# Both RMS norms of the second block: half squares, an earlier first tile, transposes inside products, and 512 wide features made by token tile

## The reference, cut to what matters

```python
def rmsnorm(x, g):
    y = x * lax.rsqrt(jnp.mean(x * x, axis=-1, keepdims=True) + 1e-6)
    return y * g

xn = rmsnorm(x, norm_mix)                 # first norm, tag (2, 1)
q, k_..., v_..., u_rnn, gates = jnp.split(xn @ w_in, cuts, axis=-1)
merged = ...                              # recurrent branch and attention branch
h = x + merged @ w_out                    # 1024 x 1024, "out"
z = rmsnorm(h, norm_mlp) @ w_mlp_in       # second norm, tag (2, 2); 1024 x 4096
return h + jnp.square(jax.nn.relu(z)) @ w_mlp_out
```

## Time and profile before

| | us |
|---|---|
| median of three runs | 1648.37 |
| the profiled execution | 1646.42 |
| its span on the core | 1644.6 |
| TensorE busy | 1554.4 (95%) |
| VectorE busy | 1031.8 (63%) |
| ScalarE busy | 796.1 (48%) |
| GpSimd busy | 230.0 (14%) |

### The profile page before, as it was taken

The page is one execution under the profiler, slowest core; times in us unless marked ns, Lnnn a source line. Parts: engine busy times, 40 slices in busy tenths (PEclk is TensorE's granted clock), DMA queues, the critical chain, the costliest instruction groups (busy, mean ns, idle before and its releaser), DMA issues.

```text
span 1644.6 us, 25103 instructions
## 1 busy us (share of the span) xinstructions
PE 1554.4 (95%) x10311; PEld 1395.9 (85%) x10311; DVE 1031.8 (63%) x1704; ACT 796.1 (48%) x1427; POOL 230.0 (14%) x189
## 2 busy tenths in 40 slices
PE   9999999898998999989899998899988799989999
PEld 6899889698986889989789986788876699979987
DVE  5765595685855675477578765455754486646643
ACT  4545445364642455444456652453446564435531
POOL 2300121211202120032021100012010040100000
PEclk9999999999999989999999999999999799989999
DMA  8633355359564533255355564455211144535553
GB/s 315 225 103 116 93 213 194 141 178 209 185 227 156 192 114 129 78 180 205 104 179 181 184 208 158 158 187 190 82 45 62 64 156 151 200 123 185 180 181 126
DMA packets 41026, 261.32 MB, mean 159 GB/s; under 512 B 4512, under 2 KB 5152, under 8 KB 14672
## 3 DMA queue, kind: packets, MB, share of 16 engines
q1 hardware_dynamic: 35600, 238.44, 42.0%
q0 software_dynamic: 2944, 15.69, 3.7%
q10 hardware_dynamic: 2368, 5.58, 0.9%
HBM read 254.98 MB, written 4.19 MB: 158 GB/s over the span
## 4 chain that ended last, share of the span: by engine, by line
PE 76%; DVE 11%; ACT 5%; issue 3%; DMA 3%; POOL 1%; ACTq 0%; DVEq 0%; POOLq 0%; SPq 0%
PE ps L482 68%; PE ps L588 3%; DVE lows L1522 3%; DMA raw<-d_wst 2%; PE ps L669 1%; ACT wh L1014 1%; ACT S L1434 1%; DVE ar L2038 1%; PE ps L690 1%; POOL sm L2220 1%; DVE S L2100 1%; PE ps L584 0%; PE ps L708 0%; DVE xTr L1541 0%; ACT xTr L1035 0%
## 5 line engine op out<-in xcount | busy, mean ns | idle before, releaser
L1522 DVE TENSOR_TENSOR lows<-raw,wh 128x1024 fp32r<-128x1024 f32 (+3 forms) x473 | 545.4, 1172 | 263.4 <-ACT wh L1014 260.8
L482 PE MATMUL ps<-xTr,wh 128*128 128x256 f32 (+1 forms) x3536 | 649.2, 286 | 11.4 <-DVE lows L1522 7.8
L482 PEld LDWEIGHTS ps<-xTr,wh 128*128 128x128 f32 (+1 forms) x3536 | 552.6, 192 | 16.5 <-issue 9.3
L1014 ACT CAST wh<-raw 128x1024 fp32r<-128x1024 f32 (+3 forms) x473 | 455.3, 990 | 191.7 <-DMA raw<-d_wst 162.4
L482 PE MATMUL ps<-xTr,lows 128*128 128x256 f32 (+1 forms) x1768 | 502.8, 284 | 0.0
L482 PEld LDWEIGHTS ps<-xTr,lows 128*128 128x128 f32 (+1 forms) x1768 | 338.7, 192 | 0.0
L482 PE MATMUL ps<-wh,arR 128*128 128x512 f32 x928 | 298.6, 401 | 4.0 <-DVE ar L1695 4.0
L482 PEld LDWEIGHTS ps<-wh,arR 128*128 128x128 f32 x928 | 176.7, 190 | 49.3 <-DVE ar L1695 5.7
L482 PE MATMUL ps<-lows,arR 128*128 128x512 f32 x464 | 185.3, 399 | 0.0
L482 PE MATMUL ps<-wh,xTr 128*128 128x512 f32 x448 | 146.0, 403 | 16.2 <-DVE xTr L1541 9.3
L482 PE MATMUL ps<-arR,wh 128*128 128x256 f32 (+1 forms) x832 | 148.4, 281 | 0.0
(11 more groups left out here) (261 smaller groups left out, 1553.7 us busy)
## 6 DMA issues: line engine op xcount, KB each, us to landing
raw<-d_wst SPq DMA_DIRECT2D x196, 1024.0 KB, 4.9
raw<-d_wst SPq DMA_DIRECT2D x24, 512.0 KB, 3.5
raw<-d_wst SPq DMA_DIRECT2D x12, 896.0 KB, 4.5
raw<-d_wst SPq DMA_DIRECT2D x8, 672.0 KB, 4.7
ar<-d_lnp POOLq DMA_DIRECT2D x5, 1024.0 KB, 5.1
raw<-d_wst SPq DMA_DIRECT2D x8, 441.0 KB, 3.5
d_scr<-PT POOLq DMA_DIRECT2D x1, 3072.0 KB, 36.0
ar<-d_par POOLq DMA_DIRECT2D x2, 1192.0 KB, 9.5
```

What stands on the lines that cost most here:

```text
L482: op = e.matmul(out, s, m, start=start and i == 0, stop=stop and i == len(pairs) - 1)
L1014: e.copy(high_of(m), raw_of(m)).then_inc(*high.done(m))
L1522: e.tensor_tensor(low_of(m), raw_of(m), high_of(m).bitcast(F32), ALU.subtract).then_inc(*low.done(m))
```

## The change

First norm: the squares are taken by halves, into two sums (scaled by 1/32 before squaring) that the variance adds. DVE interleaves tile 0's RMS norm with tile 1's layer norm; the low parts leave `rms_scaled` and are made by `stream_split` after both halves are scaled. `warm(1)` goes. ACT casts the q2 pieces before tile 0's high parts. POOL's roots follow the new order.

Second norm: tile 0's transposes stand inside the last part of `out`, before its last two row groups; `warm(2)` and `warm(5)` go. The first 512 of the 4096 wide features are made by `tokens_by_tile` ("mlp4"), tile 1's transposes inside its `tile(0)`, before the last piece. ACT copies the two results to SBUF (`mb`), and each of features 0 to 3 is then two transposes, taken alternately with the products of features 4 to 7.

TensorE and the shared definitions:

```diff
+        mb = ar[:, 0:1024].rearrange("p (i c) -> p i c", i=2)
+        mlp_order = [4, 0, 5, 1, 6, 2, 7, 3, *range(8, 32)]
...
-                def tile(i):
+                def tile(i, turn=None):
...
+                        if turn and a == 6:
+                            turn()
...
-            def down(name, key, rw, Y, ready, tail=4):
+            def down(name, key, rw, Y, ready, tail=4, turn=None):
...
                         for p in kept:
+                            if turn and i and h and p[0] == kt - 2:
+                                turn()
                             part(*p, i, h)
...
             tile(0)
-            warm(1)
             stream_turned(tag, 1, xn[1], scaled)
...
-            down(("out", 2), ("w_out_2", 0), RW, merged2, lambda k, i: (vec, "m2l", k))
             tag = (2, 2)
-            warm(2)
-            stream_turned(tag, 0, xn[0], scaled)
-            warm(5)
-            stream_turned(tag, 1, xn[1], scaled)
-            for n in range(32):
+            down(("out", 2), ("w_out_2", 0), RW, merged2, lambda k, i: (vec, "m2l", k),
+                 turn=lambda: stream_turned(tag, 0, xn[0], scaled))
+            tile = tokens_by_tile(("mlp4",), ("w_mlp_in_2", 0), span(0, 512), lambda i: x_ready(tag)[2 * i:2 * i + 2], (act, "mlp4"))
+            tile(0, turn=lambda: stream_turned(tag, 1, xn[1], scaled))
+            product.also("stock", 2, 2)
+            tile(1)
+            for n in mlp_order:
+                if n < 4:
+                    b = M.take(w, ("mlp", n), act, "relu", n)
+                    for i in range(2):
+                        w.wait_ge(act, "mlp4", i)
+                    turned(("mlp", n), [b[:, i * 128:(i + 1) * 128] for i in range(2)],
+                           [mb[:, i, n * 128:(n + 1) * 128] for i in range(2)])
+                    continue
                 features(("mlp", n), ("w_mlp_in_2", 0), 8, 128, RW, span(n * 128), X, x_ready(tag), act, "relu", n)
```

ScalarE, first norm (`squares` takes a half h of a tile now, in both norms):

```diff
             tag = (2, 1)
-            squares(tag, 0, (vec, "ln", 1, 3, 0, 1))
+            for h in range(2):
+                squares(tag, 0, h, vec, "ln", 1, 3, 0, h)
+            highs_of("q2", 0, far=0)
             stream_split(tag, 0, (product, "up", 1, 2 * NZ - 1))
-            squares(tag, 1, (vec, "ln", 1, 3, 1, 1))
-            highs_of("q2", 0, far=0)
+            for h in range(2):
+                squares(tag, 1, h, vec, "ln", 1, 3, 1, h)
```

ScalarE, second norm:

```diff
-            squares2(0)
+            first, *others = pieces.of["mlp4",]
+            highs(first, far=0)
+            for h in range(2):
+                squares(tag, 0, h, vec, "res", "out", 2, 0, h)
+            squares(tag, 1, 0, vec, "res", "out", 2, 1, 0)
             stream_split(tag, 0, (product, "g2", 1, 7))
-            squares2(1)
+            squares(tag, 1, 1, vec, "res", "out", 2, 1, 1)
+            for n in others:
+                highs(n, far=0)
             stream_split(tag, 1, (product, "g2", 1, 7))
+            n = others[-1] + 1
+            highs(n, far=pieces.splits[cast[0]] + 1 - n, count=product.at["stock", 2, 2])
+            for i in range(2):
+                w.wait_ge(product, "mlp4", i)
+                e.copy(mb[:, i, :], M["mlp4", i][:, :]).then_inc(*act.done("mlp4", i))
```

VectorE, first norm (`averaged`, `centred` and `rooted` are the layer norm's `gained` in three parts; the low halves are gone from `rms_scaled`):

```diff
+            normed(last, name, 1.0, 0)
+            for h in range(2):
+                residual(last, name, 1.0, 1, h)
             rms_var(tag, 0)
+            for h in range(2):
+                moments(last, name, 1, h)
+            averaged(last, 1)
             rms_scaled(tag, 0)
+            centred(last, 1)
+            stream_split(tag, 0)
+            rooted(last, 1)
+            lows_for("q2", 0, far=0)
             rms_var(tag, 1)
-            lows_for("q2", 0, far=0)
             rms_scaled(tag, 1)
+            stream_split(tag, 1)
```

VectorE, second norm:

```diff
+            for h in range(2):
+                residual2(0, h)
+            lows_due(others[0], far=0)
+            rms_var(tag, 0)
+            rms_scaled(tag, 0)
+            residual2(1, 0)
+            stream_split(tag, 0)
+            residual2(1, 1)
+            lows_due(others[1], far=0)
+            rms_var(tag, 1)
+            rms_scaled(tag, 1)
+            lows_due(others[2], far=0)
+            stream_split(tag, 1)
```

More of the change, by code:

```diff
@@ L1480, in scalar @@
             tag = (2, 2)
[L1482 to L1486, removed]
-            squares2(0)
+            first, *others = pieces.of["mlp4",]
[3 more added lines that the diff above has]
+            squares(tag, 1, 0, vec, "res", "out", 2, 1, 0)
             stream_split(tag, 0, (product, "g2", 1, 7))
-            squares2(1)
+            squares(tag, 1, 1, vec, "res", "out", 2, 1, 1)
+            for n in others:
+                highs(n, far=0)
             stream_split(tag, 1, (product, "g2", 1, 7))
[L1492 to L1497, removed]
+            n = others[-1] + 1
[3 more added lines that the diff above has]
+                e.copy(mb[:, i, :], M["mlp4", i][:, :]).then_inc(*act.done("mlp4", i))
+            for p, n in enumerate(mlp_order):
+                s = p % 8
+                if n < 4:
+                    w.wait_ge(cross, "mlp", n)
+                else:
+                    highs_of("mlp", n)
+                    w.wait_ge(product, "mlp", n)
+                if p >= 8:
+                    w.wait_ge(vec, "z2l", mlp_order[p - 8])
                 else:
@@ L1563, in gained, with centred @@
                 e.tensor_scalar(ve_, mv[:, 1:2], 1e-5, None, ALU.add).then_inc(*vec.done("var", *tag, i))
+            def centred(tag, i):
+                x = xt(i)
+                mv = list(norm_smalls(i))[1]
                 w.wait_ge(ln_in[tag])
@@ L1566, in gained, with rooted @@
                                        ALU.mult).then_inc(*vec.done("gain", *tag, i))
+            def rooted(tag, i):
+                x = xt(i)
+                rs = list(norm_smalls(i))[4]
                 w.wait_ge(vec, "gain", *tag, i)
@@ L1572, in gained @@
                                            ALU.add).then_inc(*vec.done("ln", *tag, i, h))
+            def gained(tag, i):
+                averaged(tag, i)
+                centred(tag, i)
+                rooted(tag, i)
             def normed(tag, name, scale, i):
@@ L1882, in vector @@
                 tag = (l, 3)
[L1883 to L1886, removed]
+                if l + 1 < DEPTH:
                     normed_by_tile(tag, ("dn", l), 1.0, ("kv", l + 1), ("stock", l, 3))
             def rms_var(tag, i):
-                ss, ve_, rs = rms_smalls(i)
+                ss, ve_, rs, s1 = rms_smalls(i)
                 w.wait_ge(act, "ss", *tag, i)
-                e.tensor_scalar(ve_, ss, 1.0 / 1024, 1e-6, ALU.mult, ALU.add).then_inc(*vec.done("rvar", *tag, i))
+                e.tensor_scalar(ve_, ss, s1, 1e-6, ALU.add, ALU.add).then_inc(*vec.done("rvar", *tag, i))
             def rms_scaled(tag, i):
@@ L2189, in vector, with residual2 @@
             tag = (2, 2)
[L2190 to L2198, removed]
-                lows_for("mlp", n)
-                for m in ([n - 1] if n else []) + ([31] if n == 31 else []):
-                    r = r_[:, m % 8, :]
+            first, *others = pieces.of["mlp4",]
+            lows_due(first, far=0)
+            def residual2(i, h):
+                xh = xt(i)[:, h * 512:(h + 1) * 512]
+                w.wait_ge(product, "out", 2, i, h)
+                e.scalar_tensor_tensor(xh, M["out", 2, i, h][:, :], 0.5, xh, ALU.mult, ALU.add).then_inc(*vec.done("res", "out", 2, i, h))
+            for h in range(2):
[11 more added lines that the diff above has]
+            stream_split(tag, 1)
+            n = others[-1] + 1
+            lows_due(n, far=pieces.splits[left[0]] + 1 - n, count=product.at["stock", 2, 2])
+            for p, n in enumerate(mlp_order):
+                if n >= 4:
+                    lows_for("mlp", n)
+                for m in ([mlp_order[p - 1]] if p else []) + ([31] if n == 31 else []):
+                    r = r_[:, mlp_order.index(m) % 8, :]
                     w.wait_ge(act, "relu", m)
@@ L2307, in gpsimd, with root, rms_root @@
                     e.dma_start(grow, lnp_d[6][:, 0:1024]).then_inc(*gain_in[2, 1].done())
-                roots((l, 3))
                 if l == 0:
+                    roots((l, 3))
                     next_gains((0, 3), 3, (1, 1))
-            def rms(tag):
-                for i in range(2):
-                    ss, ve_, rs = rms_smalls(i)
-                    w.wait_ge(vec, "rvar", *tag, i)
-                    inverse_root(rs, ve_).then_inc(*pool.done("rrs", *tag, i))
+            def root(tag, i):
+                st, mv, nm, ve_, rs, nr = norm_smalls(i)
+                w.wait_ge(vec, "var", *tag, i)
+                inverse_root(rs, ve_).then_inc(*pool.done("rs", *tag, i))
+            def rms_root(tag, i):
+                ss, ve_, rs, s1 = rms_smalls(i)
+                w.wait_ge(vec, "rvar", *tag, i)
+                inverse_root(rs, ve_).then_inc(*pool.done("rrs", *tag, i))
             def first_block_done():
```

(4 more changed lines are left out.)

31 lines of the change are left out of this document (14 added, 17 removed).

## The result

The changed kernel takes 1628.71 us (median of four, 1628.21 to 1631.80) against 1647.34 for the kernel before on the same chip (four, 1643.23 to 1649.96): a ratio of 0.989, 95% interval 0.9865 to 0.9915. That is 18.1 us less by the ratio (14 to 22). The forecast was 1625.7 us, in a range of 1621 to 1632, and 22.7 us less.

The account below looks back on a forecast made before the run. TensorE, busy 95% of the span, was taken as the bound, so only its idle, useless or slow-clock time counts. First norm -10.65 and second norm -12.05 gave -22.7 on 1646.42, 1623.7; the median's 1.95 made 1625.7 us, range 1621 to 1632.

Parts of the forecast that it names:

- First norm, -10.65: First norm, down product to the end of q2's tile 1: ends at 1038.3 against 1048.95, 10.65 us less.
- the warming as the cover: First norm: `warm(6)` holds TensorE to 1021.74 and hides tile 0's norm, with 0.9 us to spare.
- Second norm up to tile 1: Second norm, through mlp4's tile 1: ends at 1457.05, where the kernel before stood at 1470.95 after four features.
- The waits stood at the places named: mlp4's tile 0: TensorE idles 1.0 us before it, 0.95 before piece 2, 0.65 before the last piece.
- Four pairs, 0.85: Features: the 512 token-major features need four pairs of transposes, 0.21 us of TensorE each, 0.85 us added.
- The alternation's second price, 1.0: Feature loop: ACT and DVE turn in 2.98 us against TensorE's 2.88; stock used up near feature 21, 1.0 us of waits.
- the clock falls once: At one of the two norms: 6.4 us at half rate cost 3.2 us, total 1628.9; chance 0.17.
- A fall of the clock was also named as a sign of being wrong: The prediction expected granted clock 1.00 in both q2 tiles and called itself wrong if the clock falls.
- The rule weighed there: Stretches before the tiles: transposes don't count as clock activity; 2.65 and 2.8 us in the first norm, 2.0 at most in the second.
- Each pair costing a whole turn of the loop (6.9 us): Features: each transposed feature costs ACT and DVE a whole 2.98 turn, 6.9 us more, total 1632.6; chance 0.10.
- The inserted transposes had their operand: Rival, both norms: inserted transposes lack their operand and the second tile is late, 1 to 1.5 us each, 1628.4; chance 0.12.
- The weight ring: Features and final product: mlp4 holds half the four weight groups, loads land late, 24 us in all, 1650; chance 0.02.

Follow-up runs that it names:

- Experiment 1: Only the first norm's part of the change, second norm and features as in the kernel before but for squares by halves: 1633.67 us, 0.9923.
- experiment 6: The changed kernel without the six warm products after the first norm's down product: 1631.41 us, 0.9909.
- experiment 9: The changed kernel with squares by whole rows again in both norms: 1627.38 us, 0.9866.
- Experiment 7: The changed kernel with ScalarE casting the third mlp4 piece before the second half of tile 1's squares in the second norm: 1624.13 us, 0.9869.
- experiment 10: The changed kernel with VectorE squaring before low parts, third mlp4 piece cast early, four warm products, tile 0's high parts before tile 1's first squares: 1620.14 us, 0.9830.
- experiment 3: The changed kernel with VectorE squaring the previous feature before making the next low part in the feature loop: 1622.26 us, 0.9852.
- experiment 5: The changed kernel without token-major features: tile 1's transposes follow the out product, then 32 plain features: 1628.77 us, 0.9886.
- experiment 2: Only the second norm's part of the change, first norm's order as in the kernel before, squares by halves: 1637.80 us, 0.9949.

## Why the prediction was right, and where a term was not

The time fell into the range and the direction was right. But it fell there 4.6 us short of the gain that was forecast: two terms came out 0.9 better, and one 5.4 worse. The terms, in the order of the forecast (from the profiled executions):

- **First norm, -10.65: measured -10.96** (21.57 us from the down product to the end of tile 1, against 32.53). Tile 0 at 7.80 (forecast 8.0), tile 1 at 16.03 (16.3), clock 1.00, the warming as the cover: each as forecast. Experiment 1 puts 10 to 15 us on this part, experiment 6 shows what the cover is for. Half squares took 0.63 + 0.19 where 0.59 + 0.19 was taken, and experiment 9 that it didn't matter.
- **Second norm up to tile 1: 0.6 better than forecast.** From the inserted transposes to tile 1's end 16.91 us (1431.94 to 1448.85), forecast 17.55. The waits stood at the places named, but were 0.63, 0.53 and 0.48 and not 1.0, 0.95 and 0.65. Experiment 7 shows the cause of the last two and experiment 10 that of the first: ScalarE's order.
- **Four pairs, 0.85: as forecast**, 3.09 from pair to pair.
- **The alternation's second price, 1.0: this is the term that was mis-sized; it measured 6.4.** The forecast read the loop of 2.98 us against TensorE's 2.88 rightly, and said that the rest would wait "for 1.0 in all" from about feature 21 on. TensorE's ten last features do run 2.98 apart (1501.54 to 1531.33), 1.0 us. But it followed only one product of the loop, the low parts that the features need. The same loop also empties PSUM. When the features end, ScalarE is behind with two relus, TensorE turns to the final product, which wants their banks, and nothing spreads that lag any more: 2.35 us. Behind it the clock fell: 3.1 us.
- **The clock.** The rival "the clock falls once" had the right size (3.2 us against 3.1) for the wrong place, so that its 1628.9 is so near 1628.7 is luck. It was meant for the stretches ahead of the tiles, and all four of those kept full clock. A fall of the clock was also named as a sign of being wrong, and it came, at the start of the final product, where no term and no rival looked for it. The rule weighed there (the Trainium skill, "TensorE: Matmul & The Clock Gate", Part 4: PE-mode transpose: a transpose doesn't count as busy in the same way) isn't decided by these stretches, since none of them lost the clock.
- **The rivals that did not come.** Each pair costing a whole turn of the loop (6.9 us): the pairs took 4.2 us of the loop for two features, as the forecast's 1.25 has it, though the stall it feared came by the banks. The inserted transposes had their operand. The weight ring never bound: features and final product wait for no load.

By these terms -22.7 becomes -22.7 - 0.3 - 0.6 + 5.4 = -18.2. The same two traces give -17.6 from the down product to the end, and the ratio -18.1. That the terms meet the ratio to 0.1 is partly luck: they are those of the slowest of four executions, with a mean granted clock of 0.976 (0.979 to 0.981 in the others). What is not settled: in how many executions the clock falls; only profiled ones show where.

## What to carry to other kernels

A loop between two helping engines that is 3.5% slower than the engine that they serve shows as nothing while there is stock. Then it is paid turn by turn (1.0 us here), and what is left of it at once, where the main engine changes to other work (2.35 us, and the clock behind it). So price such a lag at the end of the loop, and for every resource that the loop gives back, not only for the operand that it supplies. Before a stage is tuned, look whether the order inside such a loop can be changed for nothing: here one exchanged pair of lines was worth 0 in the kernel before and 6.4 us in the changed one.

## What the runs showed of the hardware

- **A fall of the clock after short waits.** TensorE idled 0.34 us, worked for about a microsecond, idled 2.0 us, and was granted 0.50, the 1.2 GHz level, for 6.15 us. In the first norm, 1.6 us of idle behind eight transposes (2.7 us from product to product) left it at full clock each time (the changed kernel and experiments 1, 3, 5, 7 and 9). Of the five profiled executions with the same two waits at the end (the changed kernel and experiments 2, 6, 7 and 9), the clock fell in four, for 1.7 to 3.1 us of loss, and in one not at all. The kernel before and experiment 2, with the same order in the first norm, also lost different amounts there (32.5 and 35.0 us for the stage). The Trainium skill ("TensorE: Matmul & The Clock Gate", Part 1) says that the count of slow matmuls at a start differs from run to run of one kernel. These traces are of different kernels with the same stage; as far as that goes, they agree.
- **One root, three prices.** GpSimd's 128x1 root took 1.53 us beside VectorE's centring pass, 0.55 beside its statistics, and 1.02 where a scaling pass began just ahead of it.
- **A transpose runs at the granted clock.** Eight fp32 transposes in a row took 1.04 us at 1.00 and 1.97 at 0.50 (experiments 5 and 6).
- **Half a square costs more than half**: 0.63 + 0.19 us for 512 columns, 1.06 + 0.19 for 1024.
